# Token projections that stream 512 weight columns per matmul, in a decoder kernel on one core

## What is computed

```python
# first stack, layer 0 and layer 1
q, k, v, g = split(x @ w_in)               # v: [256 tokens, 1024]
y = (attention(q, k, v) * silu(g)) @ w_out
x = layer_norm(ALPHA * x + y)
# second stack
z = rms_norm(h) @ w_in_ab                  # z[:, 0:512] goes to a 2-D Fourier mix
q, k, v = z[:, 512:1024], z[:, 1024:1536], z[:, 1536:2048]
m = rms_norm(mem)
k, v = split(m @ wkv[layer])               # values of 256 memory tokens, 1024 wide
h = h + softmax(q @ k.T) @ v @ wo
```

## Time and profile before

| | us |
|---|---|
| median of 3 runs | 1078.62 |
| lowest, highest | 1078.27, 1079.88 |
| the profiled execution | 1080.66 |
| its span, first to last instruction | 1078.9 |
| TensorE busy | 1039.4 |
| VectorE busy | 693.4 |
| ScalarE busy | 535.6 |

### The profile page before, as it was taken

One profiled execution on the slowest core, in us unless ns is written; L12 is line 12 of the kernel. 1 busy time (PEld: TensorE's weight loads), 2 busy tenths in 40 slices (PEclk: granted clock), 3 DMA queues, 4 the chain that ended last, 5 costly groups with the idle time before them and its releaser, 6 DMA issues.

```text
span 1078.9 us, 19922 instructions
## 1 busy us (share of the span) xinstructions
PE 1039.4 (96%) x8144; PEld 1004.7 (93%) x8144; DVE 693.4 (64%) x1002; ACT 535.6 (50%) x822; POOL 226.1 (21%) x167
## 2 busy tenths in 40 slices
PE   8969999999999999999999999999999999999996
PEld 8959987999998899979999999899999999999996
DVE  5989976674446567646455658846576655658842
ACT  4325567365548546355435437644345545436631
POOL 3745201210004232001000103611024100102610
PEclk9979999999999999999999999999999999999998
DMA  9424532555540344515443455446545542555421
GB/s 347 154 86 146 196 118 88 186 195 195 195 162 35 121 155 178 217 58 194 167 147 109 170 190 194 154 169 245 205 164 209 181 156 81 193 190 180 148 106 39
DMA packets 26623, 173.27 MB, mean 161 GB/s; under 512 B 2880, under 2 KB 5184, under 8 KB 5952
## 3 DMA queue, kind: packets, MB, share of 16 engines
q1 hardware_dynamic: 24832, 161.26, 41.8%
q10 hardware_dynamic: 1728, 11.14, 2.7%
HBM read 167.15 MB, written 5.24 MB: 160 GB/s over the span
## 4 chain that ended last, share of the span: by engine, by line
PE 75%; DVE 13%; ACT 5%; issue 2%; POOL 2%; DMA 1%; SPq 0%; POOLq 0%; DVEq 0%; ACTq 0%
PE bank L373 63%; DVE wl L1163 5%; PE bank L479 2%; DVE work L1193 2%; DVE work L1477 2%; ACT wh L737 2%; PE bank L509 1%; POOL acc L1603 1%; DMA vec<-vecs 1%; DVE work L1480 1%; PE bank L499 1%; PE bank L441 1%; PE bank L511 1%; PE bank L600 1%; ACT work L1084 1%
## 5 line engine op out<-in xcount | busy, mean ns | idle before, releaser
L1163 DVE TENSOR_TENSOR wl<-raw,wh 128x1024 fp32r<-128x1024 f32 x300 | 394.9, 1324 | 251.0 <-ACT wh L737 249.3
L737 ACT ACTIVATE wh<-raw 128x1024 fp32r<-128x1024 f32 x300 | 312.9, 1054 | 302.9 <-PE bank L373 286.1
L373 PE MATMUL bank<-xh,wh 128*128 128x256 f32 x1312 | 367.3, 287 | 6.2 <-DVE wl L1163 4.1
L373 PE MATMUL bank<-xh,wl 128*128 128x256 f32 x1312 | 363.0, 283 | 0.0
L373 PE MATMUL bank<-xl,wh 128*128 128x256 f32 x1312 | 339.2, 284 | 0.0
L373 PEld LDWEIGHTS bank<-xh,wh 128*128 128x128 f32 x1312 | 252.1, 192 | 7.8 <-DVE wl L1163 4.8
L373 PEld LDWEIGHTS bank<-xh,wl 128*128 128x128 f32 x1312 | 252.3, 192 | 0.2
L373 PEld LDWEIGHTS bank<-xl,wh 128*128 128x128 f32 x1312 | 237.9, 192 | 0.1
L373 PE MATMUL bank<-yh,wh 128*128 128x256 f32 x768 | 210.6, 287 | 0.8 <-ACT yh L1088 0.8
L373 PE MATMUL bank<-yh,wl 128*128 128x256 f32 x768 | 208.5, 284 | 0.0
L373 PE MATMUL bank<-yl,wh 128*128 128x256 f32 x768 | 179.8, 285 | 4.2 <-POOL yl L1638 4.2
(11 more groups left out here) (156 smaller groups left out, 1307.3 us busy)
## 6 DMA issues: line engine op xcount, KB each, us to landing
raw<-w SPq DMA_DIRECT2D x149, 1024.0 KB, 4.8
k_scratch<-kt ACTq DMA_DIRECT2D x2, 1024.0 KB, 7.1
kt<-k_scratch ACTq DMA_DIRECT2D x2, 1024.0 KB, 6.3
cs<-cst SPq DMA_DIRECT2D x1, 1152.0 KB, 12.8
raw<-w SPq DMA_DIRECT2D x2, 512.0 KB, 6.3
h<-xt SPq DMA_DIRECT2D x1, 1024.0 KB, 7.2
v<-memt ACTq DMA_DIRECT2D x1, 1024.0 KB, 6.4
m_scratch<-yh ACTq DMA_DIRECT2D x1, 1024.0 KB, 6.1
```

What stands on the lines that cost most here:

```text
L373: return pe.matmul(b[:, j, :], lhs, rhs, start=k0 + k == 0 and q == 0 and (j == 0 or not both_open), stop=k0 + k == KT * p.deep - 1 and q ...
L737: act.activation(wh[:, n % 2, :, part], raw[:, n % RAW_SLOTS, :, part], ACT.Copy).then_inc(hi_ready, 1)
L1163: dve.tensor_tensor(wl[:, n % 2, :, part], raw[:, n % RAW_SLOTS, :, part], wh[:, n % 2, :, part].bitcast(F32), ALU.subtract).then_inc(lo_r ...
```

## The change

The token phases get a function of their own, `project_tokens`. A chunk now holds 512 output columns of half of the rows, instead of 256 columns of all rows; so two chunks make one block of 512 columns. Each matmul streams 512 columns into a whole bank, the tokens 0 to 127 into bank `pair`, 128 to 255 into `pair + 1`. A chunk is 2 halves x 2 token halves x 2 row tiles x 3 products = 24 matmuls. Each half chunk is awaited and given back by itself. A new semaphore `tok_full` tells that the first bank of a block is full; the second is told by `w_used`. ScalarE copies [128, 512] twice for each block, after its second chunk. Hooks of these phases are now keyed by (chunk, half, token half). Chunks lie in HBM and in the slots half by half, so that each half is 1024 adjacent numbers on a partition; the first load's two DMAs read adjacent pieces of 4 KB instead of 512 bytes. `schedule()` marks the six phases as wide; one of the six lines stands in the diff.

```diff
-    add("va", 4, "act")
+    add("va", 4, "act", wide=True)
...
-            sp.dma_start(raw[:, 0, :, 0:P], w[0][:, :, 0:P]).then_inc(first_half, 16)
+            sp.dma_start(raw[:, 0, 0, :], w[0][:, 0, :]).then_inc(first_half, 16)
             sp.dma_start(h[:, :, :], xt).then_inc(x_in, 16)
-            sp.dma_start(raw[:, 0, :, P:CW], w[0][:, :, P:CW]).then_inc(raw_full[0], 16)
+            sp.dma_start(raw[:, 0, 1, :], w[0][:, 1, :]).then_inc(raw_full[0], 16)
...
+            def project_tokens(name, oh, ol, ready=None, hooks={}, tile0=0):
+                p = PH[name]
+                enter(p)
+                for c in range(p.n):
+                    n = p.n0 + c
+                    slot = n % 2
+                    for half in range(2):
+                        pe.wait_ge(lo_ready, 2 * n + half + 1)
+                        if ready is not None and c < 2:
+                            hi_, lo_ = ready(4 * c + 2 * half)
+                            pe.wait_ge(*hi_)
+                            pe.wait_ge(*lo_)
+                        for t in range(2):
+                            if c >= 2 and c % 2 == 0 and half == 0:
+                                pe.wait_ge(evac[p.reader], p.base + c - 1 + t)
+                            for e in range(2):
+                                k = 4 * (c % 2) + 2 * half + e
+                                kk, part = tile0 + k, slice(t * P, t * P + P)
+                                for q in range(3):
+                                    mm = pe.matmul(bank[p.pair + t][:, :], (oh, oh, ol)[q][:, kk, part],
+                                                   (wh, wl, wh)[q][:, slot, half, e * 2 * CW:(e + 1) * 2 * CW],
+                                                   start=k == 0 and q == 0, stop=k == KT - 1 and q == 2,
+                                                   skip_group_check=True)
+                            if t == 1:
+                                mm.then_inc(w_used, 1)
+                            elif half == 1 and c % 2 == 1:
+                                mm.then_inc(tok_full, 1)
+                            if (c, half, t) in hooks:
+                                hooks[c, half, t]()
...
-            project("va", xh, xl, tok=True, hooks={(1, 1, 7): lambda: bcast("mem"), (2, 1, 7): first_scores,
-                                                   (3, 1, 3): second_scores})
+            project_tokens("va", xh, xl, hooks={(1, 1, 1): lambda: bcast("mem"), (2, 1, 1): first_scores,
+                                                (3, 1, 0): second_scores})
...
-            project("vb", xh, xl, tok=True, hooks={(3, 0, 3): first_logits, (3, 1, 3): lambda: z_scores(1)})
+            project_tokens("vb", xh, xl, hooks={(3, 0, 0): first_logits, (3, 1, 0): lambda: z_scores(1)})
...
+                    if p.wide and evacuate is not None:
+                        if c % 2 and c // 2 >= skip:
+                            for t in range(2):
+                                if t == 0:
+                                    act.wait_ge(tok_full, TOKBASE[name] + c // 2 + 1)
+                                else:
+                                    act.wait_ge(w_used, 2 * n + 2)
+                                evacuate(c // 2, t, bank[p.pair + t][:, :])
...
-            def va(c, b):
-                if c == 2:
+            def va(c, t, b):
+                if c == 1 and t == 0:
                     spread("mem", rb_m)
...
-                    def first_values():
-
-                        pv = PH["vx1"]
-                        act.wait_ge(w_used, 2 * pv.n0 + 2)
-                        memory_values(0, b3(pv.pair))
+                    def first_memory_values():
+                        for t in range(2):
+                            if t == 0:
+                                act.wait_ge(tok_full, TOKBASE["vx1"] + 1)
+                            else:
+                                act.wait_ge(w_used, 2 * (PH["vx1"].n0 + 1) + 2)
+                            memory_values(0, t, bank[PH["vx1"].pair + t][:, :])
```

More of the change, by code:

```diff
@@ L77, in schedule, with add @@
     order = []
-    def add(name, chunks, reader, outs=None, deep=1):
+    def add(name, chunks, reader, outs=None, deep=1, wide=False):
         nonlocal at
@@ L86, in add @@
         count[reader] += p.outs
+        p.wide = wide
         p.pair = 2 * (len(order) % 2)
@@ L104, in schedule @@
     add("kb", 4, "act")
-    add("vb", 4, "act")
+    add("vb", 4, "act", wide=True)
     add("attB", 0, "dve", 8)
@@ L142, in bases @@
     return table
+TOKBASE = bases(("va", 2), ("vb", 2), ("zf", 1), ("vn", 1), ("vx0", 2), ("vx1", 2))
 XBASE = bases(*[(u, 4) for u in ("first", "B", "mix0", "xa0", "ffn0", "mix1", "xa1", "ffn1")])
@@ L1776 @@
             chunks += cols(x["w_in_c_2"][0], 0, 3 * D)
-        chunks += cols(kv[l], D, 2 * D)
+        chunks += wide(kv[l], D, 2 * D)
         if l == 1:
```

99 lines of the change are left out of this document (47 added, 52 removed).

## The result

The changed kernel takes 1072.63 us (median of 4 executions, 1070.72 to 1073.83) where the kernel before, run beside it, takes 1078.74 (1078.27 to 1079.88). The ratio is 0.994, with a 95% interval of 0.9923 to 0.9957: 6.1 us less, with 4.6 to 8.3 as the interval. The forecast was 8.7 less, 1069.9, and its range of 1064.5 to 1076.6 holds the time. The profiled execution took 1073.83 with a span of 1072.0 at a mean granted clock of 0.986; that of before had 1078.9 at 0.984.

The account below looks back on a forecast made before the run. It took the kernel as bound by the projection matmul's pace of 0.120 us and TensorE's few waits. Terms -6.4 -1.07 -1.2 -1.1 -0.9 +1.2 +0.8 = -8.7 us took 1078.6 to 1069.9, range 1064.5 to 1076.6.

Parts of the forecast that it names:

- The pace: Six token projections: 480 matmuls of 512 columns replace 960 of 256 at 0.120 us start to start; -6.4 us.
- B: Token projections: a fixed 0.013 us per matmul, so 0.227 at 512 columns; -6.4 us, total 1069.9, chance 0.38.
- A: Token projections: equally long load and stream hinder each other, so 0.216 at 512 columns; -11.5 us, total 1066.2, chance 0.32.
- vx0: Token projection: TensorE's wait for the subtraction of chunk 1's second half goes; -1.07 us.
- zf: Token projection: two waits for a second half go, a new +0.3 wait for the diagonal comes; net -1.1 us.
- va: Token projection: second scores wait for the broadcast copy, now behind head 0's exponentials on ScalarE; +1.2 us.
- vb: Token projection: two value copies instead of one before head 2 on ScalarE, so TensorE's wait grows; +0.8 us.
- vx1: Token projection: the wait for a second half's subtraction goes, with 0.2 kept back for chunk 3; -1.2 us.
- it fits with 0.9 us: Chunk 3 of vx1: its subtraction ends near 825.9 and TensorE wants it at 826.8, so no new wait.
- First load: First weight chunk's transfers: 4 KB instead of 512-byte pieces load faster, passed on through VectorE's rotations; -0.9 us.
- Reading C: Token projections: stream slower in proportion to columns, 0.240 at 512, only waits change; -2.9 us, 1075.7, chance 0.26.
- the slower case: Token projections: 512 rounded columns run like fp32 rows at 0.43 us; +91 us, 1167 us, chance 0.04.

Follow-up runs that it names:

- the experiment: The changed kernel with three reorderings on ScalarE, among them the memory broadcast's read right behind the second copy of block 0: 1071.26 us, 1072.25 without.

## Why the prediction was right, and where it was wrong

- **The pace** decided most, as it had said, and B was right to the nanosecond: 0.227. No run shows its stream of 0.213 at 512 columns by itself or A's 0.216, and no row of before its 0.013. What the runs showed in their place is 0.120 us from start to start at 256 columns and 0.227 at 512: 0.107 for 256 columns more, and 0.013 less for one wide matmul than for two narrow ones. The weight put on it was thin, and the argument against A was only half sound: half the stationary operand, with its output rows, counts for 0.007 of the 0.013.
- **vx0 and zf**: right, -1.1 and -1.0. The second half of a chunk was in time. The diagonal in zf cost 0.2 to 0.3 as worked out.
- **va**: right in mechanism and within 0.2 in size. The order of ScalarE was read correctly, and the experiment took the wait away by that order alone. That the exponentials start sooner because of the rounding ahead of them is right only by way of VectorE, for which they wait.
- **vb**: right in mechanism, 0.3 too dear. TensorE's wait grew from 0.27 to 0.65, by 0.38, not by 0.57 and 0.14 and the shift of the phase.
- **vx1**: the step "it fits with 0.9 us" failed. It let ScalarE's queue run on as soon as chunk 1 was done and left out that the convolution's last rounding waits for GpSimd, 2.02 us by the row at 820.23. What stands behind it, the weight rounding of chunk 3, came at 820.77, 14.4 us after the start of the phase where it had been 14.6 before, so it had hardly moved up. The subtraction then took 1.94 us, not 1.3. The text had named this as what would make it wrong.
- **First load**: mis-sized, -0.9 against 1.65 by experiment in the trace and 1.7 in time. The rate of the transfers was read, the time of issuing them was not.
- **Half clock**: no step had it. In before's trace the granted clock fell at the down projections (0.50 from 700.0 to 703.0 and from 1027.5 to 1030.5 us) but not behind the layer norms (1.00 from 214 to 228 and from 398 to 412 us), and the sum took this as fixed. It differs from execution to execution: the kernel after has 0.67 and 0.72 in the windows behind its layer norms in one profile and 1.00 in both in the other, and such a stretch costs 1.5 us by the table. Between the two profiled executions of before and after the clock took 3.0 back at the layer norms and gave 1.1 at the end; how much of that the medians hold was not measured.
- **Reading C and the slower case** are out: 0.240 and 0.43 were not seen, and the wide form is no pair of 256, since a pair costs 0.240. The slower case was also priced too low: 0.43 is (3.60 - 0.59)/7, with 0.59 for the length of the last of the eight, so it is the distance of one record, and a plain fp32 matmul of 512 columns is two (the 8 records of L664 in the earlier trace rows are 4 matmuls).
- **An error of adding**: the terms of rival A sum to -13.4, not -12.4, so its time would have been 1065.2, and with va and vb at half price 1064.1, just outside the range that was to hold it. It changes nothing for reading B.

## What to carry to other kernels

Where a kernel is bound by the pace of its matmuls, read the start-to-start distance at two widths: if one of the wide takes less than two of the narrow (here 0.227 us against 0.240), fewer, wider matmuls save the difference. The wide form here gave up alternating banks, and with the halves undone TensorE waited 5.0 us for ScalarE's block copies (the rows of 3.1 and 1.9), so what stands ahead of that copy on its engine, and what that in turn waits for on a third engine, must be followed to its end before a margin is called one. When two executions of the same kernel differ, look at where the granted clock fell and what TensorE waited for just ahead; a wait that cannot be shortened can be filled, if the filler is no longer than the wait: sized so, the fillers took 2.9 us off here, and 72 that ran in no wait added 16.

## What the runs showed of the hardware

- Matmuls on rounded operands start 0.120 us apart at 256 columns and 0.227 at 512 with 128 stationary columns, and 0.113 at 256 columns with 64. At a granted clock of 0.50 those of 256 columns with 128 stationary ones start 0.213 apart (700.95 to 702.87 us in the kernel before, ten in a row).
- Idle times of 0.94 us ahead of a layer norm's sums brought half clock (granted clock 0.50 for about 3.4 us) in 10 of 20 cases, idle times of 2.12 us in the down projections in 19 of 22; the profile of the version with the halves undone has none of either. With both filled, the profiles of two versions show none there.
- Issuing a DMA with 512-byte pieces took SyncE 0.64 us instead of 0.39 with 4 KB pieces, and those queued behind it took longer too, up to 0.99 instead of 0.59 for an unchanged one.
- VectorE's subtraction of 1024 elements a partition takes 1.20 to 1.23 us with GpSimd idle and 1.2 to 2.3 beside GpSimd's work, 1.81 on average in the stretch shown.
